# Deltanet projections as three products of split parts, z turned to feature by token, and the input's remainder kept where the residual was

## The reference, cut to what matters

```
h = rms_norm(x, g_mix) * (1 + sc1) + sh1              # 512 x 1024
proj = h @ w_in                                        # 1024 x 7008 columns
dn_qkv, dn_z, dn_b, dn_a, c_q, c_kv, k_r, gates = split(proj)
# gated deltanet, 8 heads of width 128
qkv = silu(causal 5-tap convolution of dn_qkv)
o = o_fwd + o_bwd                                      # two chunked delta-rule scans
o = rms_norm(o, o_gain) * silu(z)
y_dn = o @ w_o_dn
# latent attention from c_q (512 columns), c_kv (256) and k_r (64)
merged = sigmoid(gates_dn) * y_dn + sigmoid(gates_mla) * y_mla
x = x + gt1 * (merged @ w_out)                         # then 16 experts, then a second block of 2 layers
```

## Time and profile before

| what | value |
|---|---|
| three runs | 2896.01, 2898.41 (median), 2901.75 us |
| the profiled execution | 2904.21 us, its span 2902.2 us |
| PE busy, share of the span | 2705.2 us, 93% |
| PE waiting in seven turns for `o_ready` (L1474) | 7.6 us |
| PE in one modulation slice (L1467, 290.74 us) | 1.92 us |
| TensorE's granted clock, mean of the span | 0.974 |
| DVE, ACT, POOL busy | 1089.9, 829.8, 696.8 us |
| one turn of the head loop | 71.7 us (same instruction at 206.03 and 277.72) |

### The profile page before, as it was taken

One profiled execution on the slowest core, in us unless ns is written; L12 is line 12 of the kernel. 1 busy time (PEld: TensorE's weight loads), 2 busy tenths in 40 slices (PEclk: granted clock), 3 DMA queues, 4 the chain that ended last, 5 costly groups with the idle time before them and its releaser, 6 DMA issues.

```text
span 2902.2 us, 34775 instructions
## 1 busy us (share of the span) xinstructions
PE 2705.2 (93%) x14304; PEld 2007.1 (69%) x14304; DVE 1089.9 (38%) x1800; ACT 829.8 (29%) x1444; POOL 696.8 (24%) x297
## 2 busy tenths in 40 slices
PE   7999999999989996999999699999999998999998
PEld 4777777786447884444444497878878796888877
DVE  3555555533342024121212488420014696300034
ACT  3433333333333222000000325532222326322122
POOL 2222222220013400000000132333434332343433
PEclk9999999999999997999999899999999999999999
DMA  7211112002102324999999621123222221223221
GB/s 255 52 58 58 58 58 59 35 30 80 37 29 85 123 88 149 373 409 409 409 408 409 242 88 59 59 73 102 88 102 88 80 80 44 74 87 102 89 100 44
DMA packets 212561, 382.34 MB, mean 132 GB/s; under 512 B 10833, under 2 KB 145877, under 8 KB 211413
## 3 DMA queue, kind: packets, MB, share of 16 engines
q1 hardware_dynamic: 211088, 379.06, 36.8%
q10 hardware_dynamic: 1349, 1.51, 0.2%
HBM read 378.44 MB, written 2.10 MB: 131 GB/s over the span
## 4 chain that ended last, share of the span: by engine, by line
PE 69%; DMA 8%; issue 7%; DVE 5%; PEld 5%; ACT 3%; POOL 2%; DVEq 1%; PEldq 0%; SPq 0%; ACTq 0%; POOLq 0%
PE bank L1545 14%; PE bank L1550 13%; PE bank L1549 13%; PE bank L1805 7%; DMA ring<-in_w_up 4%; DMA ring<-in_w_gate 3%; PE bank L1750 2%; PE bank L1693 2%; PEld bank L1353 2%; PE bank L1413 1%; PE bank L1422 1%; PE bank L1599 1%; PE bank L1426 1%; PE bank L1616 1%; PE bank L1319 1%
## 5 line engine op out<-in xcount | busy, mean ns | idle before, releaser
L709 POOL TENSOR_TENSOR w_lo<-ring,w_hi 128x2048 fp32r<-128x2048 f32 x96 | 444.8, 4633 | 1289.0 <-ACT w_hi L721 1289.0
L721 ACT ACTIVATE w_hi<-ring 128x2048 fp32r<-128x2048 f32 (+1 forms) x114 | 215.0, 1886 | 686.1 <-PE bank L1545 686.0
L1545 PE MATMUL bank<-hT_hi,w_hi 128*128 128x512 f32 x864 | 349.5, 404 | 11.6 <-DVE hT_lo L2571 10.0
L1549 PE MATMUL bank<-hT_lo,w_hi 128*128 128x512 f32 x864 | 342.0, 396 | 0.0
L1550 PE MATMUL bank<-hT_hi,w_lo 128*128 128x512 f32 x864 | 339.9, 393 | 0.0
L1805 PE MATMUL bank<-ring,xeT 128*64 128x512 f32 x992 | 225.5, 596 | 30.7 <-DMA ring<-in_w_gate 18.3
L2762 DVE TENSOR_TENSOR ffn_hT<-ffn_sg,bank 128x512 f32<-128x512 f32 x44 | 30.3, 689 | 461.5 <-PE bank L1550 461.5
L1545 PEld LDWEIGHTS bank<-hT_hi,w_hi 128*128 128x128 f32 x864 | 163.8, 190 | 50.4 <-DVE hT_lo L2571 10.8
L1550 PEld LDWEIGHTS bank<-hT_hi,w_lo 128*128 128x128 f32 x864 | 164.0, 190 | 41.0
L1549 PEld LDWEIGHTS bank<-hT_lo,w_hi 128*128 128x128 f32 x864 | 163.3, 189 | 35.5 <-issue 1.0
L1805 PEld LDWEIGHTS bank<-ring,xeT 128*64 128x64 f32 x992 | 77.1, 136 | 155.5 <-issue 152.9
(11 more groups left out here) (492 smaller groups left out, 5042.5 us busy)
## 6 DMA issues: line engine op xcount, KB each, us to landing
ring<-in_w_gate SPq DMA_DIRECT2D x86, 1024.0 KB, 9.1
ring<-in_w_down SPq DMA_DIRECT2D x86, 1024.0 KB, 14.1
ring<-in_w_up SPq DMA_DIRECT2D x82, 1024.0 KB, 14.1
ring<-in_w_in SPq DMA_DIRECT2D x33, 1024.0 KB, 5.4
head_w<-in_w_in SPq DMA_DIRECT2D x32, 512.0 KB, 5.3
mod_w<-in_w_mod SPq DMA_DIRECT2D x8, 2048.0 KB, 8.5
ring<-in_w_out SPq DMA_DIRECT2D x12, 1024.0 KB, 5.1
ring<-in_w_mod SPq DMA_DIRECT2D x8, 1024.0 KB, 15.3
```

The lines of the kernel that those rows point to most:

```text
L709: pool.tensor_tensor(w_lo[m % 2][:], raw[m % RAW][:], w_hi[m % 2][:].bitcast(F32), ALU.subtract).then_inc(lo_ready, 1)
L721: return act.activation(dst, src, ACT.Copy)
L1545: first = mm(dst, a[0], b[0], start=start, stop=False)
L1549: mm(dst, a[0], b[1], start=False, stop=False)
```

## The change

The input is split right after it is computed: `h_full` (in x's place), `h_hi` (in hT's place, by ACT) and `h_lo` (over `h_full`, by DVE). The small projection L1297 is done on `h_full` ahead of the first q projection, since `h_lo` is written over it. Each slice of `head_w` is split in `head_hi` (ring slots 0 and 1, by ACT) and `head_lo` (over `head_w`, by DVE), and all four projections of a head, z too, are `mm3` products with `h_hi`, `h_lo` as the moving side. z comes out feature by token; POOL multiplies it into `oT_dn` after ACT has written that, and ACT's next z silu waits for this (`gated`). The query latent's weights are loaded after the last z projection into `head_w`'s place; POOL rebuilds `h_full` as `h_hi + h_lo` between the heads 6 and 7. `h_hi` is not made again before the merge. `x` is loaded again before the experts' weights.

```diff
-            for j, c0 in enumerate((C_CQ, C_CQ + 256, C_CKV)):
-                load(N_LATENT + j, kview(N_LATENT + j), kcols(w_in, c0, 256))
+            load(N_LATENT + 2, kview(N_LATENT + 2), kcols(w_in, C_CKV, 256))
...
+            sp.wait_ge(sem("z_done"), HEADS)
+            for j in range(2):
+                load(N_LATENT + j, latent_w[j][:], kcols(w_in, C_CQ + j * 256, 256))
...
+            sp.wait_ge(sem("merge_done"), 2 * merge_place(7, False) + 2)
+            for t in range(TT):
+                sp.dma_start(x[:, t, :], A["x"][0, t * P:(t + 1) * P, :]).then_inc(sem("x_in"), 16)
--- POOL, end of a head; between heads 6 and 7
+                in_turn(pool, "z_ready", h)
+                pool.wait_ge(sem("head_done"), h + 2)
+                pool.tensor_tensor(o, o, z_silu[:], ALU.mult).then_inc(sem("gated"), 1)
+            with pool.Fori(0, HEADS - 1) as h:
+                head(h)
+            pool.wait_ge(sem("z_done"), HEADS)
+            for k in range(KD):
+                last = pool.tensor_tensor(h_full[:, k, :], h_hi[:, k, :].bitcast(F32), h_lo[:, k, :].bitcast(F32), ALU.add)
+            last.then_inc(step["h_full_ready"], 1)
+            head(HEADS - 1)
--- ACT
+            def head_part_hi(h, s):
+                if s < 3:
+                    act.wait_ge(sem("qkv_w_in"), h * 48 + 48)
+                else:
+                    act.wait_ge(sem("z_w_in"), h * 16 + 16)
+                c = slice(s * HD, (s + 1) * HD)
+                copy(head_hi[:, :, c], head_w[:, :, c]).then_inc(sem("head_w_hi"), 1)
+            for s in range(3):
+                head_part_hi(0, s)
             reached(act, "mod1_cols")
...
+            for k in range(KD):
+                act.wait_ge(sem("hT_dve"), k // 2 + 1)
+                copy(h_hi[:, k, :], h_full[:, k, :]).then_inc(step[f"h_hi_{k}"], 1)
+            head_part_hi(0, 3)
...
+                act.wait_ge(sem("gated"), h + 1)
+                act.activation(z_silu[:], bank[2][:], ACT.Silu).then_inc(once_a_turn["z_ready"], 1)
...
                 if more:
+                    head_part_hi(h + 1, 3)
                     keep_raw(h + 1, 0)
...
+                if more > 1:
+                    head_part_hi(h + 2, 0)
+                    head_part_hi(h + 2, 1)
                 act.wait_ge(sem("o_done"), h + 1)
... (squares and root of the output)
+                if more > 1:
+                    head_part_hi(h + 2, 2)
... (before the loop)
+            for s in range(3):
+                head_part_hi(1, s)
-            src_hi(h_hi, hT, range(KD))
--- PE
+            def head_slice(dst, h, s, k0, k1, first=False):
+                if k0 == 0:
+                    pe.wait_ge(sem("head_w_lo"), h * 4 + s + 1)
+                c = slice(s * HD, (s + 1) * HD)
+                for k in range(k0, k1):
+                    if first:
+                        reached(pe, f"h_lo_{k}")
+                    last = mm3(dst, both((head_hi, head_lo), every, k, c), both((h_hi, h_lo), every, k), k == 0, k == KD - 1)
+                return last
...
-                    project_z(h + 1)
+                    project(h + 1, 3)
... (latent_q, first product)
+                        reached(pe, "h_full_ready")
--- DVE
+            def head_part_lo(h, s):
+                dve.wait_ge(sem("head_w_hi"), h * 4 + s + 1)
+                c = slice(s * HD, (s + 1) * HD)
+                tt(head_lo[:, :, c], head_w[:, :, c], head_hi[:, :, c].bitcast(F32), ALU.subtract).then_inc(sem("head_w_lo"), 1)
... head_part_lo(0, 0) and (0, 1) before quarters; then
+            reached(dve, "small_done")
+            for k in range(KD):
+                reached(dve, f"h_hi_{k}")
+                tt(h_lo[:, k, :], h_full[:, k, :], h_hi[:, k, :].bitcast(F32), ALU.subtract).then_inc(step[f"h_lo_{k}"], 1)
+            head_part_lo(0, 2)
+            head_part_lo(0, 3)
... in head: head_part_lo(h + 1, 0) and (1) after g_wide, (2) after q_decT, (3) after solve_Y; then
-                in_turn(dve, "z_ready", h)
-                    stt(o_tok[:, t, :], bank[7][:, t * P:(t + 1) * P], o_scale[:, t:t + 1], z_silu[:, t, :], ALU.mult, ALU.mult)
+                    ts(o_tok[:, t, :], bank[7][:, t * P:(t + 1) * P], o_scale[:, t:t + 1], None, ALU.mult)
```

More of the change, by code:

```diff
@@ L139, in build @@
         head_w = r("head_w", [P, KD, 512])
+        head_lo = at("head_lo", HEADW_AT, [P, KD, 512], F32R)
+        head_hi = at("head_hi", 0, [P, KD, 512], F32R)
+        latent_w = [at(f"latent_w{j}", HEADW_AT + 8192 * j, [P, KD, 256]) for j in range(2)]
+        h_full = at("h_full", X_AT, [P, KD, SEQ])
+        h_lo = at("h_lo", X_AT, [P, KD, SEQ], F32R)
+        h_hi = at("h_hi", HT_AT, [P, KD, SEQ], F32R)
         conv_out = r("conv_out", [P, 3, SEQ])
@@ L1280, in _, with mm3, both @@
             first_turn(7)
-            def project_first(s):
[L1285 to L1293, removed]
+            def mm3(dst, a, b, start, stop, before=False):
+                first = mm(dst, a[0], b[0], start=start, stop=False)
+                if before:
+                    first.then_inc(parts_used, 1)
+                mm(dst, a[0], b[1], start=False, stop=False)
+                return mm(dst, a[1], b[0], start=False, stop=stop)
+            def both(ap, *idx):
+                return [part[idx] for part in ap]
+            every = slice(None)
+            def head_slice(dst, h, s, k0, k1, first=False):
[7 more added lines that the diff above has]
+                return last
+            def project_first(s):
+                head_slice(bank[FIRST_QKV[s]][:], 0, s, 0, KD, s == 0).then_inc(sem("qkv_done"), 1)
             pe.wait_ge(sem("w_small_in"), 32)
+            pe.wait_ge(sem("hT_act"), 4)
+            pe.wait_ge(sem("hT_dve"), 4)
             for t in range(TT):
                 for k in range(KD):
-                    last = mm(bank[7][:, t * 96:(t + 1) * 96], hT[:, k, t * P:(t + 1) * P], w_small[:, k, :],
+                    last = mm(bank[7][:, t * 96:(t + 1) * 96], h_full[:, k, t * P:(t + 1) * P], w_small[:, k, :],
                               start=k == 0, stop=k == KD - 1)
             last.then_inc(step["small_done"], 1)
+            project_first(0)
             project_first(1)
@@ L1317, in project @@
                     pe.wait_ge(sem("raw_ready"), h * 3 + 1)
-                for k in range(k0, k1):
-                    last = mm(bank[0 if s == 1 else 1][:], head_w[:, k, s * HD:(s + 1) * HD], hT[:, k, :], start=k == 0, stop=k == KD - 1)
+                last = head_slice(bank[(1, 0, 1, 2)[s]][:], h, s, k0, k1)
                 if k1 == KD:
-                    last.then_inc(sem("qkv_done"), 1)
+                    last.then_inc(sem("z_done" if s == 3 else "qkv_done"), 1)
             def latent_q(t, u0=0, u1=2 * KD):
@@ L1541, in project_v @@
                 last.then_inc(once_a_turn["mla_w_used"], 1)
-            def mm3(dst, a, b, start, stop, before=False):
-                first = mm(dst, a[0], b[0], start=start, stop=False)
-                if before:
-                    first.then_inc(parts_used, 1)
-                mm(dst, a[0], b[1], start=False, stop=False)
-                return mm(dst, a[1], b[0], start=False, stop=stop)
-            def both(ap, *idx):
-                return [part[idx] for part in ap]
-            every = slice(None)
             def merge(m, b, ks):
@@ L2215, in head @@
                     .then_inc(once_a_turn["g_wide_ready"], 1)
+                if more:
+                    head_part_lo(h + 1, 0)
+                    head_part_lo(h + 1, 1)
                 in_turn(dve, "len_ready", h)
@@ L2240, in head @@
                 dve.wait_ge(sem("S_ready"), h * 7 + 1)
-                tt(solve_Y[:], solve_S[:, 0], ident[:].unsqueeze(1).to_broadcast([P, TT, P]), ALU.add).then_inc(sem("eye_ready"), 1)
+                tt(solve_Y[:], solve_S[:, 0], ident[:].unsqueeze(1).to_broadcast([P, TT, P]), ALU.add).then_inc(once_a_turn["eye_ready"], 1)
+                if more:
+                    head_part_lo(h + 1, 3)
                 for lv in range(1, 7):
@@ L2399, in _ @@
                     take_rope_and_v(i + 1)
-            src_lo(h_lo, hT, h_hi, KD, range(KD))
+            src_lo(h_lo, h_full, h_hi, None, range(KD))
             for g in range(8):
                 if g == 3:
-                    src_lo(o_mla_lo, oT_mla, o_mla_hi, 2 * KD, range(KD))
+                    src_lo(o_mla_lo, oT_mla, o_mla_hi, KD, range(KD))
                 for b in range(2):
```

77 lines of the change are left out of this document (39 added, 38 removed).

## The result

| | before | after |
|---|---|---|
| median of 4 runs | 2897.38 us | 2927.11 us (2925.28 to 2930.62) |
| ratio | | 1.0101, 95% interval 1.0084 to 1.0119 |
| span of the profiled execution | 2902.2 us | 2925.7 us |
| granted clock, mean | 0.974 | 0.966 |

The change makes the kernel 1% slower. The forecast was 2901.4 us, range 2885 to 2915; the result is outside.

A forecast was written before the change was run, and what follows sets the result against it. PE, busy 93% of the span, was taken to bound the kernel unless it waits; -13.3 (loop) + 7 (preamble) + 8.8 + 1.4 (last head) - 0.9 (rest) = +3.0 us, giving 2901.4 us, range 2885 to 2915.

The forecast's parts named there:

- The products: Head loop's projections: 1.42 us less for each of q, k, v and 1.86 for z, 6.1 us a turn; most doesn't come through.
- q and the chain to `solve_Y`: k transposes to PE's restart: q gives 1.42 us, the subtraction takes 1.25, meetings on ACT and POOL add 0.3.
- The levels and last pieces of v: Six levels after `solve_Y`: shorter products worth 0; four last v products: 0.72 us a turn gained, 0 if ACT and DVE aren't ready.
- The end of a turn: Output's squares to its transposes: weights awaited before squares, 1.3 of z's 1.86 us come through, bounds 0 and 1.86.
- D: End of a turn's last q, k, v projection, 277.45 in the profile; the end of a turn was timed from it.
- The rival on the clock: Longer wait for `solve_Y` brings the lower clock into two levels: 1.5 us a turn lost, 10 us, 2912; chance 0.15.
- the rival on late weights: Turn's end: ACT's weights wait ahead of the squares, 3 us later gives 2922, half 2912; decides from 0.4 us; chance 0.2.
- The loop's bound of +7: Upper bound for seven periods between the k transposes of heads 0 and 7, forecast -13.3 us, lower bound -28.
- The preamble: Before head 0's k transposes: added splits and subtractions make them later, +6.3, taken +7 us, bounds +2 and +12.
- The last head: Before `latent_q`: POOL's rebuild of `h_full` makes PE stand 7.8 us, clock 1, +8.8; missing next q +1.4; bounds +7, +12.
- the first rival: Head loop: the subtraction in the `solve_Y` chain costs nothing, 3.4 us a turn, -10 us, 2888; chance 0.3.
- The rest: Merge and after: ACT earlier at the first split, PE's wait and slower clock go, -0.9 us; reload of x costs 0.

The follow-up runs named there:

- e2: Changed kernel with DVE's subtraction of the next v weights moved from the chain to `solve_Y` to just behind it: 2922.13 us, 1.0080 of the kernel before.
- e1: Changed kernel with ACT's two splits of the next weights moved from before the output's squares and root to behind them: 2909.42 us, 1.0030.
- e3: Changed kernel with seven useless float32r products on PE ahead of its wait for the output's scaling, in seven turns: 2919.22 us, 1.0070.
- e9: Changed kernel, ACT's order untouched, with the next q, k, v weights loaded one by one as each place comes free: 2911.04 us, 1.0036.
- e10: e1 with DVE copying the modulation slice three times instead of once before it releases the output's transposes: 2933.36 us, 1.0109.
- e7: e6 with the preamble reordered: `h_full` before weight splits, small projection by tile, earlier `g_ready`, head 1's weights loaded one by one: 2889.09 us, 0.9956.
- e5: Changed kernel with both moves, those of e1 and e2: 2906.22 us, 1.0019 of the kernel before.
- e6: e5 with `h_full` rebuilt by DVE in four pieces of 128 tokens instead of by POOL: 2898.45 us, 0.9988.
- e4: Changed kernel without POOL's rebuild of `h_full`; the latent products read `h_hi` alone, leaving out the input's remainder: 2915.05 us, 1.0049.

## Why the prediction was wrong

**The products: right.** Three instructions start 0.70 us apart (0.68 forecast), z takes 5.75 us (5.45).

**q and the chain to `solve_Y`: the prices right, the clock beside them missed.** The subtraction costs 1.07 us in K-S in the turns with the low clock (11.52 against 10.45; 1.25 forecast), and e2 gets 1.0 of it back. The table's 1.35 mixes in the turn that kept its clock. POOL's gating and the two subtractions at the turn's start do meet (DVE 3.43 us for 2.44, POOL 2.23 for 1.27). That is one after another, as the Trainium skill (SBUF — State Buffer, "SBUF: two separate sides") has it. The meeting puts the z silu 0.7 us later (3.99 us behind the output's transposes, 3.30 before). With the low clock that is hidden, as ACT still idles 1.77 us before `knT`. With the clock kept it isn't: T-K is 9.67, which q's 1.42 us and the returned clock explain against the 12.61 of before, but ACT has no idle time left and K-S is 12.9. So 1.3 of the 3.2 us that the clock gives in T-K are lost again, and my 0.3 for these meetings holds only while PE is slow.

**The levels and last pieces of v:** 0 was forecast for the levels and 0.72 us for the four pieces; 0.2 came for both together (S-U 32.26 to 32.07). No run takes them apart.

**The end of a turn: this is the step that failed.** Its own working nearly held: squares 9.85 us behind the scan's start (9.2 behind D forecast), transposes 15.6 (14.9 forecast), so that 0.63 of z's 1.86 us came through instead of 1.3. My sum let PE stand from D + 13.5 to D + 14.9 and priced that wait at its length, 1.4 us, with nothing for the clock behind it; it was 1.9 to 2.2. e1, e3, e9 and e10 show that this is the larger part: behind a wait of 2.2 us here, of 2.5 in e10, PE's granted clock goes to 0.50 for the next turn's transposes, lengths and decay rows, 3.2 us in T-K (12.86 in e10, 9.67 in e1), 1.9 once K-S has taken its part, and e10's 1.5 us of added wait cost 3.3 us a turn. The rival on the clock named the mechanism and placed it behind `solve_Y`; there the longer wait (5.0 us) left S-U where it was. The trace before had the row that would have told me: the decay rows took 3.46 us behind a wait of 1.1 us, and I did not ask what they take at 2.4 GHz (2.03 us). The Trainium skill (TensorE: Matmul & The Clock Gate, "HAM oscillation — how this bites in real kernels") says that a TensorE that waits often loses its clock again and again; the turns agree, 12.93 us in five and 9.67 in the one that kept it.

In numbers: a turn was to fall by 1.9 and rose by 0.2 us, 2.1 off: 0.9 from T to S, 0.5 from S to U, 0.7 from U to T. With the clock kept (e3) it falls by 1.2, so the clock is 1.4 of the 2.1. The 0.7 is the rival on late weights in a small dose: they were there at D + 7.9 instead of 7.2, and the squares 0.7 to 1.0 us late, above the 0.4 at which I said that it decides; it gives some 4 us in all. The loop's bound of +7 isn't the sum of the bad ends that I had written down for its parts, which is some +22 (3.1 us a turn); with the 10.2 forecast for the last head taken off, the seven periods came to +2.3, where I took -13.3.

**The preamble: the mechanism right, the size short.** +7 forecast, at most +12; it is the one segment that left its own bounds. In nine executions with this preamble head 0's k transposes came at 102.7 to 108.1, 105.4 in the mean; in two with the old one at 92.5 and 92.7. So +10 to +16. I had PE's start at 41.1 (it is 43.7, as ACT splits weights ahead of `h_full`), the small projection at 7.3 us (10.4, in part at 1.2 GHz behind a wait of 3.5), `g_ready` at 66.2 (71.6), and head 1's weights' wait nearly right (7.8 for 7.2). The low clock behind the wait for `g_ready` was in my sum. Behind the two other waits it was not: the small projection took 3.1 us more at 0.50, and from ACT's splits of head 1's weights (done at 97.8) to the k transposes it took 10.3 us instead of 8.3, with the clock at 0.50 for 98 to 104. So about 5 of the 9.3 us between 98.8 and 108.1 are the same omission, 2.6 are PE's later start, and the rest is small.

**The last head: right.** PE waits 9.0 us (7.8, and 1 for the clock, forecast); the stretch grew by 9.0, forecast 8.8 + 1.4 - 1.9 = 8.3. The other sums of the prediction come out, but for the first rival's, which leaves out the last head's 1.4: it gives 2889, not 2888.

**The rest** was to give 0.9; the profiled pair gives 4.6 behind head 7's k transposes. But that stretch, of equal code in nearly all kernels, lasted from 2303.7 to 2314.1 us in the 14 profiled executions. So nothing of it can be put down to the change, and of the span's +23.5 some 5 us either way are of this kind.

## What to carry to other kernels

Price a wait of TensorE by its length and by what its next instructions cost at the lower clock; where a profile has the same instruction at two durations, that difference is a term of the sum. Don't put a copy that waits for a DMA ahead of a chain's next step on an engine that works in order: load it slice by slice as its place comes free, or queue it behind. And before work is taken off a busy engine, take away its short waits: one signal given earlier was worth 18 us in the kernel before, where the change with its 49 us of saved products cost 30, and gained 12 only after three places in the loop and the preamble had been mended (e7).

## What the runs showed of the hardware

- The wait that PE's clock doesn't survive isn't one fixed length. At the output's transposes 1.00 us kept it in e1, e5, e6 and e9, but e7 lost it once for part of the stretch (T-K 11.33 in its first turn). Behind 1.09 us, in the kernel before, it was at 0.50 from 224.25 on, 2.2 us behind the transposes' start. Waits of 1.80 to 1.90 us kept it five times (changed kernel, e2, e4) and lost it three times (e2, e4); every one from 1.94 to 2.52 us lost it, in whole or in part, 2.21 us within 0.7 us of the start.
- A useless product was cheaper than a wait: seven of them, 1.87 us a turn, made the kernel 8 us faster.
- The preamble of one and the same code differed by up to 5.4 us between executions. Most of it lay in the small projection, 7.4 us at a granted clock of 1.00 behind a wait of 0.9 us (e1), 10.8 us with 0.50 until 48 us behind one of 1.15 us (e3); `h_lo` starts between 50.1 and 54.2.
